# Head-pair loop of a sparse-attention stage: PSUM divided by stage instead of by pair, logits issued two pairs ahead

## The reference, cut to what matters

```python
s_s = einsum('bghd,...', qg, ks) * scale + bias_s       # selected branch
p_s = masked_softmax(s_s, mask_s)
o_s = einsum('...', p_s, vs)
...
s_w = einsum('bqghd,bkgd->bghqk', qg, kw) * scale + head_bias(d_w)   # window branch
p_w = masked_softmax(s_w, mask_w)
o_w = einsum('bghqk,bkgd->bqghd', p_w, vw)
o = stack([o_c, o_s, o_w], axis=-1)
return einsum('bqhdc,bqhc->bqhd', o, gates)             # one gate for each branch and head
```

## Time and profile before

| what | value |
|---|---|
| median of 3 runs | 2757.11 us (2755.89 to 2761.37) |
| the profiled execution, its own time | 2754.71 us |
| span of its instructions | 2752.9 us |
| PE busy | 2655.4 us (96%) |
| DVE busy | 1592.7 us (58%) |
| ACT busy | 1209.9 us (44%) |
| mean granted TensorE clock | 0.989 of full speed |

### The profile page before, as it was taken

The page is one execution under the profiler, slowest core; times in us unless marked ns, Lnnn a source line. Parts: engine busy times, 40 slices in busy tenths (PEclk is TensorE's granted clock), DMA queues, the critical chain, the costliest instruction groups (busy, mean ns, idle before and its releaser), DMA issues.

```text
span 2752.9 us, 32432 instructions
## 1 busy us (share of the span) xinstructions
PE 2655.4 (96%) x12218; PEld 2192.3 (80%) x12218; DVE 1592.7 (58%) x1976; ACT 1209.9 (44%) x1491; POOL 65.0 (2%) x63
## 2 busy tenths in 40 slices
PE   7999979999999999999999987999999999999998
PEld 6888867788888888888888865888778888888886
DVE  5555776655555555565555456667465555555556
ACT  5433354444444444444333344346454444444443
POOL 0000241000000000000000000000000000000000
PEclk9999989999999999999999999999999999999999
DMA  7666406556556565655656511565456565555563
GB/s 279 184 198 189 150 1 197 160 184 198 183 183 198 180 201 183 194 182 189 192 190 197 145 62 51 195 218 195 134 173 196 186 194 187 193 188 183 195 190 118
DMA packets 248757, 482.67 MB, mean 175 GB/s; under 512 B 17208, under 2 KB 18504, under 8 KB 248040
## 3 DMA queue, kind: packets, MB, share of 16 engines
q1 hardware_dynamic: 239840, 468.25, 53.0%
q0 software_dynamic: 2672, 9.61, 1.0%
q10 hardware_dynamic: 6168, 3.76, 0.5%
HBM read 479.46 MB, written 2.13 MB: 175 GB/s over the span
## 4 chain that ended last, share of the span: by engine, by line
PE 93%; DVE 4%; ACT 2%; issue 1%; ACTq 0%; DMA 0%; DVEq 0%
PE ps_a L2112 24%; PE ps_a L2113 24%; PE ps_a L2114 24%; PE ps_b L2112 5%; PE ps_b L2113 5%; PE ps_b L2114 5%; PE ps_b L2177 1%; ACT prob L973 1%; PE ps_b L2435 1%; DVE wlo L1192 0%; PE ps_a L2558 0%; DVE prob L1867 0%; PE ps_b L2526 0%; PE ps_b L2548 0%; PE ps_a L2534 0%
## 5 line engine op out<-in xcount | busy, mean ns | idle before, releaser
L1192 DVE TENSOR_TENSOR wlo<-raw,whi 128x1024 fp32r<-128x1024 f32 x880 | 1069.2, 1223 | 812.3 <-ACT whi L544 810.5
L544 ACT CAST whi<-raw 128x1024 fp32r<-128x1024 f32 (+1 forms) x884 | 920.3, 1050 | 1163.1 <-PE ps_a L2114 921.5
L2112 PE MATMUL ps_a<-whi,xhi 128*128 128x512 f32 x2080 | 816.8, 393 | 16.2 <-DVE wlo L1192 7.6
L2113 PE MATMUL ps_a<-wlo,xhi 128*128 128x512 f32 x2080 | 812.1, 390 | 0.0
L2114 PE MATMUL ps_a<-whi,xlo 128*128 128x512 f32 x2080 | 811.9, 390 | 0.0
L2112 PEld LDWEIGHTS ps_a<-whi,xhi 128*128 128x128 f32 x2080 | 392.2, 189 | 101.8 <-issue 13.2
L2114 PEld LDWEIGHTS ps_a<-whi,xlo 128*128 128x128 f32 x2080 | 392.1, 189 | 81.7
L2113 PEld LDWEIGHTS ps_a<-wlo,xhi 128*128 128x128 f32 x2080 | 392.5, 189 | 80.0
L2112 PE MATMUL ps_a<-whi,x2hi 128*128 128x512 f32 x576 | 226.1, 392 | 0.3 <-DVE wlo L1192 0.2
L2114 PE MATMUL ps_a<-whi,x2lo 128*128 128x512 f32 x576 | 224.3, 389 | 0.0
L2113 PE MATMUL ps_a<-wlo,x2hi 128*128 128x512 f32 x576 | 224.2, 389 | 0.0
(11 more groups left out here) (344 smaller groups left out, 2048.9 us busy)
## 6 DMA issues: line engine op xcount, KB each, us to landing
raw<-in_w_in SPq DMA_DIRECT2D x108, 1024.0 KB, 5.3
raw<-in_w_up SPq DMA_DIRECT2D x108, 1024.0 KB, 5.3
raw<-in_w_down SPq DMA_DIRECT2D x108, 1024.0 KB, 5.1
raw<-in_w_gate SPq DMA_DIRECT2D x44, 1024.0 KB, 5.2
raw<-in_w_out SPq DMA_DIRECT2D x16, 1024.0 KB, 5.1
raw<-in_w_mix_out SPq DMA_DIRECT2D x16, 1024.0 KB, 5.1
raw<-in_w_mem_kv SPq DMA_DIRECT2D x8, 1024.0 KB, 11.7
raw<-in_w_br_attn SPq DMA_DIRECT2D x8, 1024.0 KB, 5.4
```

The lines of the kernel that those rows point to most:

```text
L544: return nc.scalar.copy(o, i)
L1192: return V.tensor_tensor(wlo[:, q % 4], raw[:, c % SLOTS, 2 * j:2 * j + 2], whi[:, q % 4].bitcast(F32), ALU.subtract).then_inc(lo_done, 1)
L2112: mm(o, x0, w0[:, j], start=first and j == 0, stop=False)
L2113: mm(o, x0, w1_[:, j], start=False, stop=False)
```

## The change

PSUM is divided by stage. The logits of every pair go to `ps_b` (head t in its half), the turned probabilities of every pair to banks 0, 1 and 2, and the outputs of every pair to bank 3. ACT's copy t takes bank t, DVE's single copy takes bank 2. The turning order becomes t, r. The waits follow: the logits of a head wait for the maxima of the pair before, the turning waits for the copies of the pair before, and the outputs wait for the sum of the pair before. The new orders are, for one pair x:

```diff
         def branch_logits(x, t, r, b):
 
             c = t * 1024 + (r * S if b else 2 * S + r * P)
-            return pair_bank(x)[:, c:c + (S if b else P)]
-
-        def pair_bank(x):
-            return ps_a if x % 2 else ps_b
+            return ps_b[:, c:c + (S if b else P)]
...
+            def branch_turned(x):
+
+                for t in range(2):
+                    act.wait_ge(nb["pt"], 2 * x + t + 1)
+                    copy(probt[:, x % 2].rearrange("p (r c) -> p r c", r=2)[:, :, t * S:(t + 1) * S],
+                         bank(t).rearrange("p (r s) -> p r s", r=2)).then_inc(nb["pt_act"], 1)
...
             for x in range(8):
-                for r in range(2):
-                    if x < 7:
-                        branch_exps(x + 1, r)
-                    act.wait_ge(nb["pt"], 2 * x + r + 1)
-                    copy(probt[:, x % 2, r * 768:r * 768 + 512], pair_bank(x)[:, r * 512:(r + 1) * 512]).then_inc(nb["pt_act"], 1)
...
+                if x < 7:
+                    for t in range(2):
+                        branch_exps(x + 1, t)
+                branch_turned(x)
+                if x:
+                    branch_hi(x - 1)
...
-            def branch_maxima(x):
+            def branch_maxima(x, t):
 
                 if x >= 2:
 
-                    dve.wait_ge(nb["pt"], 2 * (x - 1))
...
+                    dve.wait_ge(nb["pt"], 2 * (x - 2) + t + 1)
+                dve.wait_ge(nb["logits"], 2 * x + t + 1)
...
             def turned(x):
 
-                for r in range(2):
-                    dve.wait_ge(nb["pt"], 2 * x + r + 1)
-                    V.tensor_copy(probt[:, x % 2, r * 768 + 512:(r + 1) * 768], pair_bank(x)[:, 1024 + r * 512:1280 + r * 512]
-                                  ).then_inc(nb["pt_dve"], 1)
+                dve.wait_ge(nb["pt"], 2 * x + 2)
+                V.tensor_copy(probt[:, x % 2].rearrange("p (r c) -> p r c", r=2)[:, :, 512:768].rearrange("p r (t s) -> p t r s", t=2),
+                              bank(2).rearrange("p (t r s) -> p t r s", t=2, r=2)).then_inc(nb["pt_dve"], 1)
...
-            branch_maxima(0)
+            for t in range(2):
+                branch_maxima(0, t)
             dve.wait_ge(ns["oc"], 1)
             V.tensor_copy(cmp_o[:].rearrange("p x s -> p (x s)"), ps_a[:, :]).then_inc(ns["cmp"], 1)
-            weights(0)
+            branch_maxima(1, 0)
             c0, q0, _ = seg["br"]
             for x in range(8):
+                weights(x)
+                if x:
+                    turned(x - 1)
                 if x < 7:
-                    branch_maxima(x + 1)
-                turned(x)
-                if x < 7:
-                    weights(x + 1)
-                outputs(x)
+                    branch_maxima(x + 1, 1)
                 if x:
-                    outputs_lo(x - 1)
+                    outputs(x - 1)
+                if x < 6:
+                    branch_maxima(x + 2, 0)
+                if x >= 2:
+                    outputs_lo(x - 2)
+            turned(7)
+            outputs_lo(6)
+            outputs(7)
...
             def branch_qk(x):
-                if x == 1:
-                    pe.wait_ge(ns["cmp"], 1)
-                if x >= 2:
-
-                    pe.wait_ge(nb["y"], x - 1)
                 for t in range(2):
+                    if x:
+
+                        pe.wait_ge(nb["max"], 2 * (x - 1) + t + 1)
...
+            def branch_turn(x):
+
+                for t in range(2):
+                    pe.wait_ge(nb["diag"], x + 1)
+                    if x:
+                        pe.wait_ge(nb["pt_act"], 2 * (x - 1) + t + 1)
+                        pe.wait_ge(nb["pt_dve"], x)
+                    for r in range(2):
...
+            def branch_pv(x):
+
+                pe.wait_ge(nb["pt_act"], 2 * x + 2)
+                pe.wait_ge(nb["pt_dve"], x + 1)
+                if x:
+                    pe.wait_ge(nb["y"], x)
+                o = bank(3)
...
+            pe.wait_ge(ns["cmp"], 1)
+            pe.wait_ge(ns["vdup"], 1)
+            for x in range(8):
+                if x:
+                    branch_pv(x - 1)
+                branch_turn(x)
+                if x < 6:
+                    branch_qk(x + 2)
+            branch_pv(7)
```

More of the change, by code:

```diff
@@ L974, in branch_exps, with branch_hi @@
                 ins.then_inc(nb["exp"], 1)
+            def branch_turned(x):
[3 more added lines that the diff above has]
+                         bank(t).rearrange("p (r s) -> p r s", r=2)).then_inc(nb["pt_act"], 1)
+            def branch_hi(x):
+                act.wait_ge(nb["y"], x + 1)
+                copy(xhi[:, x], stage_t[:, x % 2, 0:S]).then_inc(nb["hi"], 1)
             for t in range(2):
@@ L979, in _ @@
             for x in range(8):
-                for r in range(2):
-                    if x < 7:
-                        branch_exps(x + 1, r)
-                    act.wait_ge(nb["pt"], 2 * x + r + 1)
-                    copy(probt[:, x % 2, r * 768:r * 768 + 512], pair_bank(x)[:, r * 512:(r + 1) * 512]).then_inc(nb["pt_act"], 1)
[L985 to L991, removed]
+                if x < 7:
[4 more added lines that the diff above has]
+                    branch_hi(x - 1)
+            act.wait_ge(nb["pv"], 7)
+            for k in range(4):
+                hi(q0 + k, chunk=c0 + k // 2)
+            branch_hi(7)
             linear("br", 0, 2, kchunks=2, opened=4)
@@ L1854, in _ @@
                             gain2_t[:, G_POOL:G_POOL + 8].unsqueeze(2).to_broadcast([P, 8, S]), ALU.mult).then_inc(ns["pooled"], 1)
-            def branch_maxima(x):
+            def branch_maxima(x, t):
                 if x >= 2:
-                    dve.wait_ge(nb["pt"], 2 * (x - 1))
-                for t in range(2):
-                    dve.wait_ge(nb["logits"], 2 * x + t + 1)
-                    for r in range(2):
[L1865 to L1872, removed]
+                    dve.wait_ge(nb["pt"], 2 * (x - 2) + t + 1)
+                dve.wait_ge(nb["logits"], 2 * x + t + 1)
+                for r in range(2):
+                    for b in range(SB):
+                        y = branch_row(x, t, r, b)
+                        ins = V.tensor_tensor_reduce(branch_prob(x, t, r, b), branch_logits(x, t, r, b),
+                                                     bias[:, 2 * x + t, (0 if b else P):S], 1.0, 3 * NEG, ALU.add, ALU.max,
+                                                     accum_out=s_bmax[:, y:y + 1])
+                link(ins)
+                y = branch_row(x, t, 0, 0)
+                V.tensor_scalar(s_bneg[:, y:y + 4], s_bmax[:, y:y + 4], -1.0, None, ALU.mult).then_inc(nb["max"], 1)
             def weights(x):
@@ L1900, in outputs @@
                     r = slice(t * HD2, (t + 1) * HD2)
-                    ins = V.tensor_tensor(stage_t[r, x % 2, 0:S], pair_bank(x)[r, t * S:(t + 1) * S], cmp_o[r, x], ALU.add)
+                    ins = V.tensor_tensor(stage_t[r, x % 2, 0:S], bank(3)[r, t * S:(t + 1) * S], cmp_o[r, x], ALU.add)
                 ins.then_inc(nb["y"], 1)
@@ L2568, in branch_qk @@
             def branch_qk(x):
-                if x == 1:
-                    pe.wait_ge(ns["cmp"], 1)
-                if x >= 2:
-                    pe.wait_ge(nb["y"], x - 1)
                 for t in range(2):
+                    if x:
+                        pe.wait_ge(nb["max"], 2 * (x - 1) + t + 1)
                     r = slice(t * HD2, (t + 1) * HD2)
                     c = t * 1024
-                    mm(pair_bank(x)[:, c:c + 2 * S], nqt[r, x, P:S], nkt[r, x // 2].rearrange("p r s -> p (r s)"), start=True, stop=True)
-                    mm(pair_bank(x)[:, c + 2 * S:c + 3 * S], nqt[r, x, 0:P], nkt[r, x // 2, :, 0:P], start=True, stop=True
+                    mm(ps_b[:, c:c + 2 * S], nqt[r, x, P:S], nkt[r, x // 2].rearrange("p r s -> p (r s)"), start=True, stop=True)
+                    mm(ps_b[:, c + 2 * S:c + 3 * S], nqt[r, x, 0:P], nkt[r, x // 2, :, 0:P], start=True, stop=True
                        ).then_inc(nb["logits"], 1)
@@ L2588, in _ @@
             ins.then_inc(ns["oc"], 1)
[L2589 to L2596, removed]
+            branch_qk(1)
+            def branch_turn(x):
[4 more added lines that the diff above has]
+                        pe.wait_ge(nb["pt_dve"], x)
+                    for r in range(2):
                         for b in range(SB):
                             for k in range(b + 1):
-                                c = r * 512 + t * S + b * P if k == 0 else 1024 + r * 512 + t * P
-                                ins = mm(ps[:, c:c + P], branch_prob(x, t, r, b)[:, k * P:(k + 1) * P],
-                                         diag[:, x % 2, 4 * t + 2 * r + b], start=True, stop=True)
-                    ins.then_inc(nb["pt"], 1)
-                if x == 0:
-                    pe.wait_ge(ns["vdup"], 1)
-                o = ps[:, 0:512]
+                                if k == 0:
```

(10 more changed lines are left out.)

## The result

The changed kernel takes 2781.74 us (median of 4 runs, 2778.84 to 2783.88) against 2756.50 us for the kernel before (4 runs): ratio 1.0087, 95% interval 1.0074 to 1.0100. It is slower by 25 us. The profiled execution has 2778.84 us and a span of 2777.0 us, 24.1 us more in each than before.

A forecast was written before the change was run, and what follows sets the result against it. The pair loop was taken as bound by a circle's latency, PE waiting through DVE and ACT. A new PE-DVE circle (+4.5 us) and seven clock falls (15 us) made +19.5 us, 2776 us as a median, range 2761 to 2785.

The forecast's parts named there:

- a fall in each round: Pair loop: the main forecast, each fall of the clock costing 1.2 to 2.7 us, 2766 to 2781 us, chance 0.68.
- the circle: Pair loop: PE and DVE wait for each other in turn, 11.0 us a round, 10.65 for the first two.
- the clock: Pair loop: seven long PE waits of about 4 us each bring a fall to half clock, 15 us in all.
- The other terms at full clock: Around and over the rounds: start +1.3, six rounds +3.7, turning 6 to 7 -1.2, end +0.7 us.
- I take 2.1 us: Pair loop: the cost of one fall of the clock, taken between two measured ones of 1.65 and 2.3 us.
- ACT off the circle: Pair loop: ACT's exponentials, 3.6 us, run beside PE's 5.3 us of outputs and turning and delay nothing.
- What would show it: Profile after: seven PE waits of about 4 us, those ahead of outputs put down to DVE's copy; 13 us rounds with falls.
- No fall: Rival, pair loop: the clock stays at 1.00 and only the circle counts, about 2761 us, chance 0.11.
- Falls that run into each other: Rival, pair loop: a fall reaching into the next wait holds on, 3.3 us each, 2784 us, chance 0.15.
- Faster: Rival, pair loop: PE and DVE run beside each other, 6.9 us a round, about 2737 us, chance 0.05.
- Turning 6 to turning 7: End of the pair loop: no further logits or maxima between, about 6.5 us against 7.8, given as -1.2 us.
- No effect: Rival, pair loop: a round takes what it took and the clock stays, 2757 us, chance 0.01.

The follow-up runs named there:

- fill4: Changed kernel with four extra products on PE ahead of the outputs of pairs 0 to 5, three ahead of the first turning: 2766.07 us, ratio 1.0023.
- turned_weights: Changed kernel with only DVE's list reordered: weights(0) ahead of maxima(1), then per round both maxima, outputs, outputs_lo, turned(x), weights(x+1): 2737.19 us, ratio 0.9931.
- one_ahead: turned_weights with logits one pair ahead instead of two, PE doing outputs(x-1), logits(x+1), turning(x): 2773.60 us, ratio 1.0059.
- turned_first: Changed kernel with DVE's copy turned(x) moved ahead of maxima(x+2, t=0), nothing else: 2749.69 us, ratio 0.9971.
- fill2: Changed kernel with two extra products on PE ahead of the outputs and one ahead of the first turning: 2771.95 us, ratio 1.0052.
- one_ahead_copies: one_ahead with ACT's copies(x) placed between the exponentials(x+1) of the two heads instead of behind all: 2754.10 us, ratio 0.9994.

## Why the prediction was right, and where it was off

Right was the sign and the mechanism: +19.5 us were forecast, +24.1 came in the profiled execution and +25.2 in the medians, with 2781.74 us inside the range of 2761 to 2785. The narrower span of the forecast with a fall in each round, 2766 to 2781, it misses by 0.7 us. Of the 4.6 us between 19.5 and 24.1, 1.8 are the circle and its ends and 2.8 the clock.

- **The circle.** Forecast were 11.0 us for a round at full clock; fill4 shows 11.2. The missing 0.2 is the outputs: their first piece takes 1.10 us behind a wait, in fill4 as before (the earlier trace rows have 1.13), and the sum had the 0.86 of the earlier trace rows, so that they take 2.8 us and not 2.6. The rest of the sum holds: 4.3 us from a turning to the maxima behind the logits (1656.61 to 1660.91; 2.7 + 1.7 forecast), and from there to the outputs 4.1 (1660.91 to 1664.99). The three semaphores of the outputs cost little, 0.10 us from the end of DVE's copy to the first of them in the changed kernel. The copy of four pieces, the one operation without a row of its own, took 0.68 us, as the plain copy of its size.
- **The other terms at full clock**, from fill4: the first turning lies 11.25 us behind the first logits, 9.95 before (+1.3, as forecast); the six rounds take 66.9 us (+5.3; +3.7 forecast, as the first two are 11.2 and 10.9 long and not 10.65); turning 6 to 7 takes 6.6 us (forecast 6.5); from turning 7 to the first product behind are 8.9 us against 8.2 (+0.7, as forecast). Together +6.3 where the sum had +4.5.
- **The clock.** Forecast was one fall for each of seven waits, and seven came. The term that was mis-sized is "I take 2.1 us": it measured 2.5 us (17.8 / 7). Each fall lasted 6.83 us with 4.9 to 5.7 under work, so half of that was lost. The fall behind the one wait of the same length in the earlier trace rows was also 6.7 us long, but had only 4.6 us of work in it, as PE waited again there; and I averaged it with the shorter one behind the loop. The step that was missing is how much work a fall holds: 6.83 us less the 1.1 to 1.9 us of it that lay in the wait. Half of what is left is 2.5 to 2.9 us; all of it under work would have been 3.4, close to the prediction's upper bound of 3.3.
- **The Trainium skill's figure** (TensorE: Matmul & The Clock Gate, section "HAM oscillation — how this bites in real kernels"), 1.67 us throttled per round, would by the prediction's estimate have given +10 us. Here 4.9 to 5.7 us of work behind each wait ran at half clock; the pattern is as the page has it, a fall in every round, and the measurement decides on the size.
- **ACT off the circle** held: its exponentials are nowhere on the chain in the rounds.
- **What would show it.** Seven waits of about 4 us came, but only one of the six ahead of outputs is put down to DVE's copy; the timeline had to show it for another.
- **The rivals.** "No fall" is refuted by the trace (0.50 in each round), and fill4, which takes the falls away, lands at its loop. "Falls that run into each other" did not happen: between two falls the clock was back at full each time. The row that it leaned on, 9.7 us at 0.50 in the earlier trace rows, had no further wait in it, since PE was busy for all 9.70 us. Its price of 3.3 us for a fall was further off than mine (2.5 measured), and yet its 2784 us lies nearer to 2781.74 than my 2776: that is luck, as the circle was too short in both sums. "Faster" was wrong for the order in the change, and its arithmetic right for another one: 6.9 us a round and about 2737 us were given for engines that run beside each other, and turned_weights does 6.95 us and 2737.2 us.
- **Slips in the sum.** Turning 6 to turning 7 is given as -1.2 us, where its terms (2.7 + 1.1 + 2.6 against 7.8) make -1.4; measured are 6.6 us against 7.7, so -1.0. "No effect" is counted with "faster" in the chances. Neither changes the forecast.

## What to carry to other kernels

When stages are set one further ahead, write down for each engine where every step stands in its list and follow the hand overs once around: here PE's outputs waited for a copy that stood behind a step that waited for PE, and the two engines took turns. Order a list by when its inputs are ready, the shortest step that the busiest engine waits for first; one line moved was worth 34 us of loop here. And count the waits that a change gives PE in length, not only in sum: four microseconds of waiting cost 2.5 us more in products at half clock, and filling a wait with products that nobody needs won that back. Taking the wait away by the order won more: 69.5 us of loop against 93.6.

## What was not expected of the hardware

- Which waits of PE were followed by a fall. Over these traces, in the loop and directly behind it: every one of 2.9 us and more was (2.88 us behind the loop of the kernel before, and 15 of 3.06 to 4.21 us in the changed kernel, one_ahead and turned_first), none of 1.6 us or less was, and of those between 1.8 and 2.6 us some were and some were not, of equal length in one execution (fill2: four of seven; one_ahead_copies: two of five).
- A fall was either about 3.4 or about 6.8 us long in and behind the loop. At the eight waits of about 4 us (seven in the changed kernel, one in turned_first) it began inside the wait and was always the longer one; at the seven of 3.1 to 3.3 us in one_ahead it was now the one, now the other.
- The profile can hide or misname who an output with three semaphores waits for. Five of the six waits of 4 us ahead of outputs are put down to "issue". The wait of 1.1 us ahead of the outputs of pair 6 is put down to ACT's copy, which ended at 1714.67, though PE started at 1715.19 and DVE's copy `turned` ended at 1715.09. The timeline of the other engines has to be read for it.
